# Two-block transformer on one core: the modulation products of block two, formed by GpSimd, with TensorE summing over the partitions

## The reference, cut to what matters

```python
def first_block(...):
    for l in range(DEPTH):                      # DEPTH = 2
        x = x + 0.5 * swiglu(rmsnorm(x, ffn1_norm[l]), ffn1_w_gu[l], ffn1_w_down[l])
        x = x + hybrid_mixer(rmsnorm(x, mix_norm[l]), ...)
        x = x + 0.5 * swiglu(rmsnorm(x, ffn2_norm[l]), ffn2_w_gu[l], ffn2_w_down[l])
    return rmsnorm(x, final_norm)

def adaln(cond, w, b):                          # w: 1024 x 6144 for each layer of block two
    return jnp.split(jax.nn.silu(cond) @ w + b, 6, axis=-1)

def layer(x, ctx, c, c_ctx, w_ada, b_ada, ...):
    sh1, sc1, gt1, sh2, sc2, gt2 = [m[:, None, :] for m in adaln(c, w_ada, b_ada)]
    csh1, csc1, cgt1, csh2, csc2, cgt2 = adaln(c_ctx, w_ada, b_ada)
    ...
```

## Time and profile before

| | us |
|---|---|
| median of 3 runs (2633.23 to 2633.75) | 2633.55 |
| the profiled execution, its own time | 2637.17 |
| its span | 2635.4 |
| TensorE busy in the span | 2597.9 (99%) |
| VectorE busy | 1412.5 (54%) |
| ScalarE busy | 528.1 (20%) |
| GpSimd busy | 7.3 (0%) |

### The profile page before, as it was taken

One profiled execution on the slowest core, in us unless ns is written; L12 is line 12 of the kernel. 1 busy time (PEld: TensorE's weight loads), 2 busy tenths in 40 slices (PEclk: granted clock), 3 DMA queues, 4 the chain that ended last, 5 costly groups with the idle time before them and its releaser, 6 DMA issues.

```text
span 2635.4 us, 51104 instructions
## 1 busy us (share of the span) xinstructions
PE 2597.9 (99%) x21966; PEld 2358.8 (90%) x21966; DVE 1412.5 (54%) x2409; ACT 528.1 (20%) x1121; POOL 7.3 (0%) x17
## 2 busy tenths in 40 slices
PE   8999999999999999999999999999999999999999
PEld 8999777889999999877888999869996799967999
DVE  6674254315766766244331766346672566535665
ACT  2111132111111111123210111331113411133110
POOL 0000000000000000000000000000000000000000
PEclk9999999999999999999999999999999999999999
DMA  6664322146555555421125556423444144431443
GB/s 264 222 220 180 120 84 78 65 159 219 199 213 220 195 221 209 160 101 68 57 105 208 214 218 225 172 92 133 163 174 159 45 158 176 173 128 65 160 161 113
DMA packets 52529, 414.98 MB, mean 157 GB/s; under 512 B 4080, under 2 KB 6384, under 8 KB 32080
## 3 DMA queue, kind: packets, MB, share of 16 engines
q1 hardware_dynamic: 48256, 357.96, 37.0%
q10 hardware_dynamic: 3456, 50.33, 5.2%
q0 software_dynamic: 592, 3.41, 0.3%
HBM read 410.64 MB, written 1.05 MB: 156 GB/s over the span
## 4 chain that ended last, share of the span: by engine, by line
PE 95%; DVE 2%; ACT 1%; DMA 1%; DVEq 1%; issue 0%; ACTq 0%; SPq 0%
PE units L820 31%; PE spots L820 23%; PE units L745 14%; PE units L941 7%; PE spots L1131 2%; PE units L1242 2%; PE spots L801 2%; PE units L1289 2%; PE units L1407 1%; PE units L919 1%; PE units L912 1%; DMA context_keys<-cond 1%; PE spots L1338 1%; PE spots L1319 1%; PE spots L1328 1%; ACT probabilities L1476 1%
## 5 line engine op out<-in xcount | busy, mean ns | idle before, releaser
L820 PE MATMUL units<-normed,weights 128*128 128x128 f32 x2176 | 270.5, 278 | 13.5 <-DMA weights<-stream 8.6
L820 PEld LDWEIGHTS units<-normed,weights 128*128 128x128 f32 x2176 | 257.3, 194 | 17.1 <-issue 16.8
L820 PE MATMUL spots<-normed,weights 128*128 128x128 f32 x2176 | 265.7, 275 | 0.2
L820 PEld LDWEIGHTS spots<-normed,weights 128*128 128x128 f32 x2176 | 254.3, 192 | 0.6 <-ACT normed L1476 0.3
L745 PE MATMUL units<-normed,weights 128*128 128x256 f32 x1040 | 230.6, 382 | 2.2 <-ACT normed L1476 2.2
L745 PEld LDWEIGHTS units<-normed,weights 128*128 128x128 f32 x1040 | 197.9, 191 | 32.4 <-issue 5.9
L1476 ACT ACTIVATE mla_q_rope<-units 128x256 f32<-128x256 f32 (+1 forms) x248 | 95.3, 387 | 529.1 <-PE units L820 488.3
L941 PE MATMUL units<-normed,weights 128*128 128x256 f32 x832 | 193.6, 387 | 0.0
L2106 DVE TENSOR_TENSOR delta_new_values<-spots,mla_q_rope 128x256 f32<-128x256 f32 x116 | 49.2, 424 | 266.0 <-PE spots L820 266.0
L941 PEld LDWEIGHTS units<-normed,weights 128*128 128x128 f32 x832 | 155.7, 191 | 29.3 <-issue 8.0
L820 PE MATMUL units<-hidden,weights 128*128 128x128 f32 x1472 | 180.9, 276 | 0.0
(11 more groups left out here) (371 smaller groups left out, 3535.1 us busy)
## 6 DMA issues: line engine op xcount, KB each, us to landing
weights<-stream SPq DMA_DIRECT2D x138, 2048.0 KB, 7.8
weights<-stream SPq DMA_DIRECT2D x48, 1024.0 KB, 5.2
values_mla_qk_mla_values<-stream ACTq DMA_DIRECT2D x24, 2048.0 KB, 8.0
weights<-stream SPq DMA_DIRECT2D x16, 768.0 KB, 6.4
constants<-consts SPq DMA_DIRECT2D x1, 1094.5 KB, 16.5
residual<-x_in SPq DMA_DIRECT2D x1, 1024.0 KB, 4.8
weights<-stream SPq DMA_DIRECT2D x4, 256.0 KB, 5.3
conv_in<-ctx_in POOLq DMA_DIRECT2D x1, 1024.0 KB, 8.5
```

What stands on the lines that cost most here:

```text
L820: mm = pe.matmul(dst[:, m * P:m * P + P], weights[:, m, kt, :], moving(kt), start=(first and m == 0 and kt == 0), stop=(kt == n - 1), skip ...
```

## The change

The 32 matmuls of a modulation step become eight. GpSimd does what stood in the other 24: it multiplies each of the eight blocks of the weights by the condition's value of each partition, once into `ada_low` and `ada_high` (in `hidden` and `delta_qkv`, for the first condition) and once in place (for the second), and then adds the eight products in three steps of 2048, 1024 and 512 columns, for each condition. The two results, 128 x 512 each, lie in `ada_part`. TensorE sums them over the partitions with a stationary side `pick`, 32 columns of zeros with a one in column 0 or 1. The weights are asked for by GpSimd instead of ScalarE: the next group as soon as the second condition's adds have read the last one. The units behind which the step stands move: `ADA_AT` and `ADA_FIRST` change. The constant angles and a few small tiles move to other places in memory, since `delta_qkv` and `hidden` are now used. The load of block two's tables waits for the last modulation group of turn two.

```diff
-ADA_AT = (1, 4, 7, 10, 13, 16)
-ADA_FIRST = (3, 5, 8, 10, 13, 16)
+ADA_AT = (3, 6, 8, 11, 13, 16)
+ADA_FIRST = (4, 7, 9, 11, 14, 16)
...
+        pick = sb("condition_columns", [P, 64])
...
+        ada_part = qkv[:, 8:12, :].rearrange("p (j a) t -> p j (a t)", j=2)
+        ada_low, ada_high = (t.rearrange("p a t -> p (a t)") for t in (hT[:, 24:32, :], qkv[:, 0:8, :]))
...
+            def load_ada(c, i):
+
+                if i == ADAS:
+                    pool.wait_ge(*merged_made.at(c, 4))
+                elif i:
+                    pool.wait_ge(*ada_read.at(c, i))
...
+                pool.dma_start(vqv[:, :], stream[bass.ds(c.turn * size + places_["ada", i], P * FULL)].rearrange(
+                    "(p w) -> p w", p=P)).then_inc(ada_loaded.handle, 16)
+
+            def halved(low, high, dst):
+
+                for n in (4, 2, 1):
+                    if n == 1:
+                        return pool.tensor_tensor(dst, low[:, 0:512], low[:, 512:1024], ALU.add)
+                    other = high if n == 4 else low[:, n * 512:2 * n * 512]
+                    pool.tensor_tensor(low[:, 0:n * 512], low[:, 0:n * 512], other[:, 0:n * 512], ALU.add)
+                    pool.drain()
+
+            def ada_parts(c, i):
+
+                pool.drain()
+                pool.wait_ge(*ada_loaded.at(c, 16 * (i + 1)))
+                if i == ADAS:
+                    pool.wait_ge(*p1_done.at(c, FFN_MU + 1))
+                for kt in range(KD):
+                    half = ada_low if kt < 4 else ada_high
+                    pool.tensor_scalar(half[:, kt % 4 * 512:kt % 4 * 512 + 512], vqv[:, kt * 512:kt * 512 + 512],
+                                       cond_s[:, kt, 0:1], None, ALU.mult)
+                pool.drain()
+                for kt in range(KD):
+                    w = vqv[:, kt * 512:kt * 512 + 512]
+                    pool.tensor_scalar(w, w, cond_s[:, kt, 1:2], None, ALU.mult)
+                pool.drain()
+                if i:
+                    pool.wait_ge(*spot_ready.at(c, SPOT["one"]["ada", i - 1][0][0] + 1))
...
+                halved(vqv[:, 0:2048], vqv[:, 2048:4096], ada_part[:, 1, :]).then_inc(ada_read.handle, 1)
+                if i != ADAS - 1:
+                    load_next(c, i)
+                halved(ada_low, ada_high, ada_part[:, 0, :]).then_inc(ada_made.handle, 1)
+                if i == ADAS - 1:
+                    load_next(c, i)
...
             def ada_sums(c, i):
 
                 banks = free_spot(c, ("ada", i))
-                pe.wait_ge(cond_made, 1)
-                pe.wait_ge(*ada_loaded.at(c, 16 * (i + 1)))
-                for kt in range(KD):
+                pe.wait_ge(pick_made, 1)
+                pe.wait_ge(*ada_made.at(c, i + 1))
+                for j in range(2):
+                    part_ = ada_part[:, j, :].rearrange("p (m c) -> p m c", m=4)
                     for q in range(4):
-                        w = vqv[:, kt * 512:kt * 512 + 512].rearrange("p (m c) -> p m c", m=4)[:, :, 32 * q:32 * q + 32]
-                        mm = pe.matmul(banks[32 * q:32 * q + 32, 0, 0:P], cond_s[:, kt, :], w, start=(kt == 0),
-                                       stop=(kt == KD - 1))
+                        mm = pe.matmul(banks[32 * q:32 * q + 32, 0, 0:P], pick[:, 32 - j:64 - j], part_[:, :, 32 * q:32 * q + 32],
+                                       start=(j == 0), stop=(j == 1))
                 mm.then_inc(spot_ready.handle, 1)
...
-                    if c.sec == "one" and k in ada_units(c, which) and (which or k != ada_units(c, which)[-1]):
-                        i = ADAS * which + ada_units(c, which).index(k) + 1
-                        if i < 2 * ADAS:
-                            load_ada(c, i)
...
```

More of the change, by code:

```diff
@@ L372, in build @@
         ctx_res = conv_flat[:, 1024:1024 + KD * T].rearrange("p (k t) -> p k t", k=KD)
-        ctx_rstd, ctx_part = row[:, 0, :], qkv[:, 9, :]
-        angle = qkv[:, 0:5, :]
+        ctx_rstd, ctx_part = row[:, 0, :], hT[:, 23, :]
+        angle = [cossin[:, 1, :], cossin[:, 0, :]] + [conv_flat[:, KD * T + T * i:KD * T + T * i + T] for i in range(3)]
         cur_of = {"ctx": cur[:, :], "twoa": row[:, 5, 0:48], "two": cur[:, :]}
@@ L702, in _ @@
-            pool.dma_start(ctx_res, ctx_in).then_inc(ctx_here, 16)
-            pool.dma_start(vec_b, vec2[0]).then_inc(vec_b_here.handle, 16)
+            def load_ada(c, i):
[3 more added lines that the diff above has]
+                    pool.wait_ge(*ada_read.at(c, i))
+                elif c.turn:
+                    pool.wait_ge(*ada_read.at(Place("one", c.turn - 1), ADA_TURN))
+                else:
+                    pool.wait_ge(*p1_done.at(c, 1))
+                places_, size = STREAM["one"]
+                pool.dma_start(vqv[:, :], stream[bass.ds(c.turn * size + places_["ada", i], P * FULL)].rearrange(
+                    "(p w) -> p w", p=P)).then_inc(ada_loaded.handle, 16)
@@ new lines, in load_next @@
+            def load_next(c, i):
+                if i + 1 < ADA_TURN:
+                    load_ada(c, i + 1)
+                elif c.turn + 1 < DEPTH:
+                    load_ada(Place("one", c.turn + 1), 0)
+            pool.dma_start(vec[:, :], vec1[0]).then_inc(vec_here.handle, 16)
+            load_ada(Place("one", 0), 0)
+            pool.wait_ge(cond_made, 1)
+            for l in range(DEPTH):
+                c = Place("one", l)
+                for i in range(ADA_TURN):
+                    ada_parts(c, i)
+                    if i == ADAS:
+                        pool.wait_ge(*normed.at(c, 3 * KD))
+                        if l + 1 < DEPTH:
+                            pool.dma_start(vec[:, :], vec1[bass.ds(l + 1, 1)].rearrange("a p v -> (a p) v")
+                                           ).then_inc(vec_here.handle, 16)
+                        else:
+                            pool.dma_start(ctx_res, ctx_in).then_inc(ctx_here, 16)
+                            pool.dma_start(vec_b, vec2[0]).then_inc(vec_b_here.handle, 16)
@@ L1559, in multiply @@
                         keep_c1(k + 1)
-                    if c.sec == "one" and k in ada_units(c, which) and (which or k != ada_units(c, which)[-1]):
-                        i = ADAS * which + ada_units(c, which).index(k) + 1
-                        if i < 2 * ADAS:
-                            load_ada(c, i)
-                        elif not last_layer(c):
-                            load_ada(Place("one", c.turn + 1), 0)
-                    if (c.sec, c.turn, which, k) == ("one", 0, 0, 0):
-                        load_ada(c, 0)
                     if (c.sec, c.turn, which, k) == ("one", 0, 0, ROTARY_AT + 2):
@@ L2619, in _ @@
             ve.memset(ones[:, :], 1.0).then_inc(ones_made, 1)
+            ve.memset(pick[:, :], 0.0)
+            ve.drain()
+            ve.memset(pick[:, 32:33], 1.0).then_inc(pick_made, 1)
             for l in range(DEPTH):
```

55 lines of the change are left out of this document (21 added, 34 removed).

## The result

The changed kernel took 3044.6 us (median of four runs, 3041.5 to 3047.5), the kernel of before 2633.65 beside it: a ratio of 1.1554, 95% interval 1.1539 to 1.1568. The forecast was 2803 us, with a range of 2655 to 2985. Its sign was right; the loss is 411 us and not 169.

A forecast was written before the change was run, and what follows sets the result against it. TensorE, busy 99% of the span, was taken as the bound. 2635.4 us of span less 33.8 saved plus 203 of VectorE holds gave 2804.6, less 1.8 about 2803 us; range 2655 to 2985.

The forecast's parts named there:

- The saving: In TensorE's 24 modulation steps, 48 records fewer save 1.41 us a step, 33.8 us in all.
- The price of an addition: GpSimd's additions take 8.0 us for one condition, 16.0 us for both.
- The hold of VectorE: GpSimd's instructions block VectorE's two-input ones whole in the feed-forward layers, costing 203 us net; chance 0.50.
- the price of a multiplication: GpSimd's multiplication of 512 columns costs the copy's pitch, 0.56 us, so sixteen take 9.0 us a group.
- The third rival: GpSimd becomes the bound, TensorE waiting at the modulation step: some 46 us a group, 2883 us; chance 0.15.
- The rest: ScalarE's lost issues, GpSimd's small loads queueing behind its work, and moved constants were costed at nothing.
- What was to show it: Signs of holds: VectorE maxima of several microseconds, GpSimd busy over 500 us, mixers and block two as long as before.
- the sign of the rival: GpSimd as the bound would show as TensorE's idle time in front of the modulation step, L868.

The follow-up runs named there:

- e7: The changed kernel without GpSimd's arithmetic, its first load of modulation weights waiting for TensorE's second unit instead of its first; 2606.8 us, ratio 0.9892.
- e4: The changed kernel with each of GpSimd's multiplications replaced by a copy of the same 512 columns; 2868.0 us, ratio 1.0887.
- e2: The changed kernel with GpSimd's multiplications left out and its additions kept, on zeros; 2812.3 us, ratio 1.067.
- e3: The changed kernel with GpSimd's additions replaced by fills and its sixteen multiplications a group kept; 2729.2 us, ratio 1.0355.
- e5: The changed kernel with 48 extra matmuls on tiles of ones ahead of TensorE's wait at 20 of the 24 modulation steps; 3060.9 us, ratio 1.162.
- e1: The changed kernel with all GpSimd multiplications and additions left out, two fills in their place; 2615.5 us, ratio 0.9923.
- e12: The changed kernel with 20 of the 24 loads of modulation weights asked for by ScalarE instead of GpSimd; 3068.5 us, ratio 1.1647.
- e9: e3 with the multiplications taking a fixed 0.5 instead of the value read per partition; 2674.3 us, a single run.
- e8: e3 with four multiplications of 2048 columns instead of sixteen of 512; 2822.0 us, a single run.

## Why the prediction was right in sign and wrong in size

**The saving** was right: 33.5 us in e7 for 33.8.

**The price of an addition** was right: 4.50 us for 2048 columns, 2.34 for 1024, 1.26 for 512, which is 8.1 us for a condition with nothing in between, where 8.0 was taken; with VectorE's holds it is 9.0 at the mean. The Trainium skill (GPSIMD Engine Reference, 3.1 Elementwise) has 4497 ns for the first, and the trace agrees.

**The hold of VectorE** was right in kind and nearly in size. L2009 (now L2053) ran up to 5.54 us where 1.2 is its own time; L2141 (now L2185) went from a median of 692 ns to 1004, L2155 (now L2199) from 292 to 540. As TensorE's idle time it is 188 us in e4, 3 of it in the opening, against 203. The two parts of the sum were not equally good. The forecast gave the additions 10.9 us and the multiplications 3.9 in an up unit; e2 and e3 show the first dear (139.8 us more idle time) and the second, at 512 columns and alone, next to nothing; that it stays so beside the additions is not shown, and e4 over e2 speaks against it.

**The failed step is the price of a multiplication**: "A multiplication by a value per partition also reads one tile, so I take the copy's pitch: 16 x 0.56 = 9.0 us a group." It is 1.55 us with VectorE out of the way (6.18 / 4) and 1.82 to 1.89 at the mean, 28 to 30 us a group, three times the price; e4, with the forecast's copies in its place, gives 176 of the 411 us back and takes away every wait for GpSimd at L868. A copy had been the nearest row, but it was taken as the answer with no bound above it, while the addition beside it had been given one. With it fell "With 25 us of work and up to 4 us of waiting GpSimd keeps up": the group takes 48 to 58 us against an interval of 31. The third rival named this mechanism and its place, L868, but with the same 9 us; its 46 us a group (its own terms make 40 to 45) and its top of 2985 were short by that. TensorE's modulation steps now start 50.0 us apart at the mean of a layer's five intervals, and 31.1 in e7. In four layers that is 378 of the 435 us that the kernel stands over e7; the other 57 lie in front of a layer's first step and behind its last. The steps are a little closer than GpSimd's issues, because GpSimd has a group ready when a layer's first step comes.

With the measured durations the forecast's own way of summing gives the group: 28.0 of multiplications, 18.1 of additions and 4.7 for the load are 50.8 of the 52.0 us.

**The clock was not in the sum.** Behind fourteen of the nineteen waits for GpSimd (8.6 to 27.3 us) the modulation products take 1.08 us where those of the other ten steps take 0.64, and in the step shown the product behind them runs at half speed and the next one partly. Slower products come to 79.4 us over the kernel, and 71.5 in e4, 5.6 of them from the opening. In the changed kernel that is hardly a cost of its own: in e5 20 us of it came back and the time did not, since GpSimd sets the pace; in e4, where VectorE stops TensorE in many waits of at most 9 us, it stands on the path: 187.6 + 71.5 make the 259.1 over e7. It is the largest part of why even the kernel that the forecast summed came out at 2868 and not at 2803.

**"The rest"** had two gaps. It counted the small loads, at nothing, and left out the first load of weights, which, moved ahead from 25.2 to 12.6 us, delayed the condition and cost 8.7 us (e1 against e7). And a load issued by GpSimd is followed by 2.6 to 5.7 us (3.5 at the mean, not the 3 to 4.4 of the expectation of e12) in which GpSimd stands still, 73.5 us over the kernel; that stands in the idle time ahead of L719 and in no row of before that the forecast read.

**What was to show it** came as written for the holds (L2053 and L2074 with long maxima, GpSimd busy over 500 us, mixers and block two as before), and so did the sign of the rival, idle time in front of L868, which outweighed the waits for VectorE 274 to 73.

## What to carry to other kernels

An engine that gets work which stands on another's schedule has to be priced in the pace of a group against the interval of whoever comes for it, with every operation at its own measured price; the nearest row of another operation was a floor here and no price, and past the interval what a group takes more was paid nearly in full (e3 against e9). A stall on a path that is full is paid as idle time and again as slower products behind it: here 0.2 to 0.5 us for each microsecond of waiting (the table's last column by the one before). And before 24 matmuls (48 records of 29 ns) are moved anywhere, compare them with what they become: 1.4 us of TensorE became 46 us of GpSimd.

## What the runs showed of the hardware

- GpSimd's multiplication of a float32 tile by a value per partition took 1.55 us for 512 columns and 5.45 for 2048, 2.7 to 3.0 ns a column, more than its addition of two tiles (1.26 and 4.50 us) and 2.5 times its copy of 512 columns (0.61 us); by each further column it is 2.5 ns against 0.82. A fixed value saves 0.08 us of 1.56 (e9). The Trainium skill (GPSIMD Engine Reference, 4.1 Engine selection) calls one-input operations "roughly line-rate"; the copy, at 0.82 ns a further column beside the 1.2 of VectorE's sums of two tiles, is in line with that; the multiplication is not, and the measurement decides.
- An addition of 2048 columns stops a VectorE instruction with two SBUF inputs to its end (55.26 to about 59.8); a multiplication of 2048 columns lets go 1.5 us before it ends (e8), and sixteen of 512 cost VectorE far less than four of 2048, though they take no less time. Why was not found. It is not only instructions with two tiles that are stopped: two of L1967 in e2, one tile by a value per partition, 0.62 us otherwise, took 5.17 beside the addition at 939.33, and TensorE's longest wait of that run, 12.0 us, stands behind them.
- A 2 MB load issued by GpSimd is followed, one addition later, by 2.6 to 5.7 us in which GpSimd starts nothing; where ScalarE issued it the same place was 0.1 us (e12).
- A 2 MB load asked for at 12.6 us, beside the first weights, made a 128 KB load asked for 8.5 us earlier on another queue land 5 us later (21.4 us from issue to landing where it was 16.4).
